# First loads in another order, a table of roots loaded at once, and the first product put between the transposes

## The reference, cut to what matters

```python
def rms_norm(x, g):
    xf = x.astype(jnp.float32)
    y = xf * lax.rsqrt(jnp.mean(xf * xf, axis=-1, keepdims=True) + EPS)
    return (y * g.astype(jnp.float32)).astype(x.dtype)
...
        h = rms_norm(x, norm_mix_pre[l])
        proj = h @ w_in[l]
        q, k, v, u, gates = jnp.split(proj, splits, axis=-1)
        q = q.reshape(b, s, ATTN_HEADS, HEAD_DIM)
        k = k.reshape(b, s, ATTN_HEADS, HEAD_DIM)
```

## Time and profile before

| | us |
|---|---|
| median of 3 runs | 1713.24 |
| lowest and highest | 1712.49, 1714.06 |
| the profiled execution, its own time | 1714.25 |
| its span, first to last instruction | 1712.4 |
| PE busy | 1585.0 (93%) |
| PE weight loads | 1120.9 (65%) |
| DVE busy | 723.9 (42%) |
| ACT busy | 532.1 (31%) |
| POOL busy | 164.0 (10%) |

### The profile page before, as it was taken

One profiled execution on the slowest core, in us unless ns is written; L12 is line 12 of the kernel. 1 busy time (PEld: TensorE's weight loads), 2 busy tenths in 40 slices (PEclk: granted clock), 3 DMA queues, 4 the chain that ended last, 5 costly groups with the idle time before them and its releaser, 6 DMA issues. The chain is left out here.

```text
span 1712.4 us, 19999 instructions
## 1 busy us (share of the span) xinstructions
PE 1585.0 (93%) x7970; PEld 1120.9 (65%) x7970; DVE 723.9 (42%) x1235; ACT 532.1 (31%) x911; POOL 164.0 (10%) x169
## 2 busy tenths in 40 slices
PE   4999899898999999998999788969999999999969
PEld 4766588788888888876766676744445444543449
DVE  4343422445444444476555676432122222212363
ACT  4333422244423323343454467221111111100242
POOL 0012201001111111102200210021000000000000
PEclk8999999999999999998999999989999999999989
DMA  6011222212221322312100221538999999999811
GB/s 253 31 68 55 101 109 99 101 60 111 83 93 71 123 99 74 114 71 98 50 25 29 95 99 50 204 154 335 419 421 421 421 421 420 418 418 421 352 39 47
DMA packets 44846, 302.85 MB, mean 177 GB/s; under 512 B 5056, under 2 KB 7232, under 8 KB 9680
## 3 DMA queue, kind: packets, MB, share of 16 engines
q1 hardware_dynamic: 42624, 294.12, 43.1%
q0 software_dynamic: 2128, 7.42, 1.3%
HBM read 299.43 MB, written 2.10 MB: 176 GB/s over the span
## 5 line engine op out<-in xcount | busy, mean ns | idle before, releaser
L580 DVE TENSOR_TENSOR w_lo<-M,w_hi 128x2048 fp32r<-128x2048 f32 x73 | 167.6, 2301 | 216.7 <-ACT w_hi L575 216.7
L2264 PE MATMUL bank<-M 128*64 128x512 f32 x1024 | 227.5, 595 | 5.7 <-DMA M<-in_w 4.7
L575 ACT ACTIVATE w_hi<-M 128x2048 fp32r<-128x2048 f32 x73 | 138.9, 1910 | 175.5 <-PE bank L748 63.6
L748 PE MATMUL bank<-HTH,w_hi 128*128 128x512 f32 x432 | 168.9, 391 | 5.2 <-DVE M L1266 5.2
L748 PE MATMUL bank<-HTL,w_hi 128*128 128x512 f32 x432 | 168.8, 391 | 0.0
L748 PE MATMUL bank<-HTH,w_lo 128*128 128x512 f32 x432 | 168.7, 390 | 0.0
L2264 PEld LDWEIGHTS bank<-M 128*64 128x64 f32 x1024 | 72.5, 137 | 139.9 <-issue 138.7
L770 PE MATMUL bank<-w_hi,HTH 128*128 128x512 f32 x256 | 106.3, 415 | 19.4 <-DVE M L1482 5.3
L2281 PE MATMUL bank<-M 128*64 128x512 f32 x512 | 113.8, 595 | 2.2 <-DMA M<-in_w 2.2
L770 PE MATMUL bank<-w_hi,HTL 128*128 128x512 f32 x256 | 102.7, 401 | 0.0
L770 PE MATMUL bank<-w_lo,HTH 128*128 128x512 f32 x256 | 102.6, 401 | 0.0
(11 more groups left out here) (312 smaller groups left out, 2940.3 us busy)
## 6 DMA issues: line engine op xcount, KB each, us to landing
M<-in_w SPq DMA_DIRECT2D x192, 1024.0 KB, 10.4
M<-in_wd SPq DMA_DIRECT2D x78, 1024.0 KB, 4.8
M<-in_nb SPq DMA_DIRECT2D x4, 1536.0 KB, 7.1
X<-in_x SPq DMA_DIRECT2D x4, 512.0 KB, 7.5
M<-in_rows POOLq DMA_DIRECT2D x4, 512.0 KB, 5.7
M<-in_tb POOLq DMA_DIRECT2D x8, 256.0 KB, 4.0
rowb<-in_rows POOLq DMA_DIRECT2D x4, 512.0 KB, 4.1
out<-M SPq DMA_DIRECT2D x16, 128.0 KB, 1.8
```

The source lines that it names most:

```text
L575: e.activation(hi[:, :], slots[slot_of[n]], ACT.Copy).then_inc(split_hi_done, 1)
L580: e.tensor_tensor(lo[:, :], slots[slot_of[n]], hi[:, :], ALU.subtract).then_inc(split_lo_done, 1)
L748: m = e.matmul(out[:, :], w[:, k0 + k, n0:n0 + 128], v[k], start=(k == 0 and i == 0), stop=(k == len(hi) - 1 and i == 2))
L2264: m = e.matmul(b[64 * s:64 * s + 64, :], Xe[:, 4 * kh + k, o + C * s:o + C * s + C], unit_w(key, 4)[:, k, :], start=(kh == 0 and k == 0), ...
```

## The change

There are four edits, all in the first stage.

- **Loads.** eps is moved next to the identity, and these 129 columns get a load of their own, right behind x0, with a semaphore of their own (`d_ident`). The first unit of weights is issued behind x1 and the second behind x3, ahead of the rest of `cst` and of `cols`. POOL issues the row of gains, then waits for x3, and only then issues the bias tables, `wpg`, `rows` and `wr`.
- **Table.** DVE sets a column to 1, and ACT takes its root ahead of everything else.
- **Order on ACT and DVE.** The stagger is written out: tiles 0 and 1 start together, the split of the first unit stands between the copies of tile 0 and those of tile 1, and tiles 2 and 3 come behind.
- **Order on PE.** Tiles 0 and 1 are transposed, then the q half of tokens 0 to 255 is made, then tiles 2 and 3 are transposed, then come the k half and the second half of the tokens. The banks of q and k are claimed ahead of those of tiles 2 and 3.

```diff
@@ sync, first loads
             for t in range(TT):
                 e.dma_start(X[:, t, :], x_d[t * 128:(t + 1) * 128, :]).then_inc(d_x[t], 16)
+                if t == 0:
+                    e.dma_start(cst[:, 0:NFIRST], cst_d[:, 0:NFIRST]).then_inc(d_ident, 16)
                 if t == 1:
-                    e.dma_start(cst[:, :], cst_d).then_inc(d_cst, 16)
-                    e.dma_start(cols[:, :], cols_d).then_inc(d_cols, 16)
+                    load_dense(e, 0)
+            load_dense(e, 1)
+            e.dma_start(cst[:, NFIRST:], cst_d[:, NFIRST:]).then_inc(d_cst, 16)
+            e.dma_start(cols[:, :], cols_d).then_inc(d_cols, 16)
...
         def first_loads_pool(e):
             load_gain(e, 0)
-            e.dma_start(wpg[:, :, :], wpg_d).then_inc(d_wpg, 16)
+            e.wait_ge(d_x[TT - 1], 16)
             for h in range(3):
                 load_tb(e, h)
+            e.dma_start(wpg[:, :, :], wpg_d).then_inc(d_wpg, 16)
...
+        one = stat()
+        FIRST_ACT = ((0, 0), (1, 0), (0, 3), "split", (1, 3), (2, 0), (3, 0), (2, 3), (3, 3))
+        FIRST_DVE = ((0, 1), (1, 1), (0, 4), "split", (1, 4), (2, 1), (3, 1), (2, 4), (3, 4))
+
         def pre_act(e):
-            for t, s in stagger(TT, 5, 2):
-                if t == 2 and s == 0:
+            e.wait_ge(one_set, 1)
+            act_own.mark(e.activation(one, one, ACT.Sqrt))
+            for step in FIRST_ACT:
+                if step == "split":
                     split_act(e, 0)
-                norm_act(e, 0, t, s)
+                else:
+                    norm_act(e, 0, *step)
             split_act(e, 1)
             split_act(e, 2)
...
         def pre_dve(e):
-            for t, s in stagger(TT, 5, 2):
-                if t == 2 and s == 1:
+            e.memset(one, 1.0).then_inc(one_set, 1)
+            for step in FIRST_DVE:
+                if step == "split":
                     split_dve(e, 0)
-                norm_dve(e, 0, t, s)
+                else:
+                    norm_dve(e, 0, *step)
...
         def pre_pe(e):
-            e.wait_ge(d_cst, 16)
-            for t in range(TT):
-                norm_pe(e, 0, t)
+            e.wait_ge(d_ident, 16)
+            norm_pe(e, 0, 0)
+            norm_pe(e, 0, 1)
...
             for half in range(2):
+                ts = slice(half * 256, (half + 1) * 256)
                 ht_ready(e, 0, 2 * half)
                 ht_ready(e, 0, 2 * half + 1)
-                gemm3_T_part(e, ("in", 0), outs, slice(half * 256, (half + 1) * 256), half == 1)
+                for j, (b, fills) in enumerate(outs):
+                    m = gemm3_T_some(e, ("in", 0), b, j, ts)
+                    if half:
+                        m.then_inc(fills, 1)
+                    elif j == 0:
+                        norm_pe(e, 0, 2)
+                        norm_pe(e, 0, 3)
```

More of the change, by code:

```diff
@@ L54 @@
 _o = 0
-for _n, _w in (("ident", 128), ("tri", 128), ("ones", 128), ("iota", 64), ("thr", 8), ("cnt", 64),
-               ("cos", 128), ("sin", 128), ("eps", 1)):
+for _n, _w in (("ident", 128), ("eps", 1), ("tri", 128), ("ones", 128), ("iota", 64), ("thr", 8), ("cnt", 64),
+               ("cos", 128), ("sin", 128)):
     CST[_n] = (_o, _w)
     _o += _w
-NCST = _o
+NCST, NFIRST = _o, 129
 def ffn_order():
@@ L221, in build @@
         d_x = [sem(f"d_x{t}") for t in range(TT)]
-        d_cst, d_cols, d_wpg, d_rows, d_rowb, d_wr, d_pT = (
-            sem(n) for n in ("d_cst", "d_cols", "d_wpg", "d_rows", "d_rowb", "d_wr", "d_pT"))
+        d_ident, d_cst, d_cols, d_wpg, d_rows, d_rowb, d_wr, d_pT = (
+            sem(n) for n in ("d_ident", "d_cst", "d_cols", "d_wpg", "d_rows", "d_rowb", "d_wr", "d_pT"))
         d_tb = [sem(f"d_tb{i}") for i in range(3)]
@@ L230, in build @@
         r_sq, r_sqrt, r_y, xadd = (sem(n) for n in ("r_sq", "r_sqrt", "r_y", "xadd"))
-        d_gain = sem("d_gain")
+        d_gain, one_set = sem("d_gain"), sem("one_set")
         u_zero, pooled, mix_hi = sem("u_zero"), sem("pooled"), sem("mix_hi")
@@ L251, in build @@
         for t in range(TT):
+            if t == 2:
+                for name in ("q", "k"):
+                    ps.put((name, 0))
             for h in range(2):
                 ps.put(("n", 0, t, h))
-        for name in ("q", "k"):
-            ps.put((name, 0))
         ATT = [(h, qt) for h in range(8) for qt in range(4)]
@@ L763, in gemm3_T_part, with gemm3_T_some @@
                     m.then_inc(fills, 1)
+        def gemm3_T_some(e, key, out, j, ts):
+            wh, wl = parts(key, KD)
+            for k in range(KD):
+                for i, (w, src) in enumerate(((wh, HTH), (wh, HTL), (wl, HTH))):
+                    m = e.matmul(out[:, ts], w[:, k, j * 128:(j + 1) * 128], src[:, k, ts],
+                                 start=(k == 0 and i == 0), stop=(k == KD - 1 and i == 2))
+            return m
         def gemm3_tok(e, key, j, t, out):
@@ L2443, in _ @@
                 first_loads_sp(e)
-                for n in range(NDENSE - 2):
+                for n in range(2, NDENSE - 2):
                     load_dense(e, n)
@@ L2806, in _layout @@
     one = np.ones((128, 1))
-    cst = np.concatenate([np.eye(128), np.triu(np.ones((128, 128)), 1), np.ones((128, 128)),
+    cst = np.concatenate([np.eye(128), one * EPS, np.triu(np.ones((128, 128)), 1), np.ones((128, 128)),
                           one * np.arange(64)[None, :], one * (C * (1 + np.arange(8)))[None, :], one * cnt,
-                          by_tok(np.cos(ang)), by_tok(np.sin(ang)), one * EPS], axis=1).astype(np.float32)
+                          by_tok(np.cos(ang)), by_tok(np.sin(ang))], axis=1).astype(np.float32)
     wr = np.concatenate([i["w_rg_2"][0], i["w_re_2"][0]], axis=1).reshape(8, 128, 36).transpose(1, 0, 2)
```

## The result

The changed kernel takes 1703.61 us (median of 9 runs, 1702.34 to 1711.82) against 1713.26 for the kernel before (9 runs, 1711.51 to 1721.20): ratio 0.9944, interval 0.9927 to 0.9962, which is 9.65 us less (6.5 to 12.5). Timed again (5 runs against 9), the ratio was 0.9960 (0.9946 to 0.9975), 6.9 us less (4.3 to 9.3).

What follows compares the result with a forecast made beforehand. The first stage up to the copy of k was taken to bound the start, with the gain row landing last. That copy moves from 41.5 to 35.4, so 1713.24 - 6.1 = 1707.1 us, range 1704.0 to 1710.6.

Steps and rivals of the forecast that it cites:

- The transfers: First loads: identity lands at about 4.9, x1 at 5.6, gain row at 8.45, first weights at 11.0 instead of 18.02.
- S: Start of tile 0's scaling on DVE, forecast at 8.5, right after the gain row lands.
- ACT and DVE: Norm and weight split ahead of the product: tile 0 scaled from 8.5, first matmul at 18.15 instead of 28.05.
- P: Start of the first matmul of the q and k product on PE, forecast at 18.15 instead of 28.05.
- PE, the step that failed: Product to k copy: first group 4.9, 16 transposes 3.5, three fast groups 8.64; k copied at 35.4.
- K: Start of DVE's copy of k, after which attention starts; forecast at 35.4 instead of 41.5, 6.1 us less.
- early rival: First stage: gain row lands with x1 (6.5), split waits for weights at 11.0, clock never falls; 1703.6, chance 0.06.
- No cost of the moves: First loads and banks: POOL's wait, later constants and swapped banks delay nothing; tables cost zero unless 14 us later.
- Passed through: After the copy of k: nothing later is tied to the program's start, so the whole 6.1 us reaches the end.
- identity no earlier: First loads: small load no quicker than the old table, ACT starts at 9.33, all 2.6 later; 1709.7, chance 0.04.
- given back: Later stages: expert weights arrive at a fixed rate, the gain ends in PE's wait for them; 1713.2, chance 0.04.
- slower: First loads: one queue's loads served side by side, first weights land at 24.5; 5.9 slower, 1719.1, chance 0.03.

Runs made afterwards that it cites:

- POOL at once: Changed kernel with POOL's wait for x3 and its new order of `wpg` taken back; k copied at 34.31 us in its profile, no whole time given.

## Why the prediction was wrong, point by point

- **The transfers**: first weights forecast at 11.0, landed at 10.7 to 11.8 in the four profiles of the changed kernel. The identity was forecast at 4.9 and was there at 4.3 in the first profile, 0.3 behind x0 (issued at 0.75, 3.3 to landing). Gain row forecast to end last, at 8.45: it did, S 8.49 on average. x1 was forecast at 5.6 and landed at 8.3 to 9.3: wrong. In the kernel before it was there at 5.4, issued 0.5 sooner and with the rate at 377 GB/s up to 5 us; here the rate was 221 from 4 to 5 us and 295 from 5 to 6. That this is the cause is likely, not shown. It cost nothing, as DVE waits for the gain row first.
- **ACT and DVE**: P was forecast at 18.15, S + 9.65; it came at S + 9.48, at 17.97 on average. Each step of that chain, with its length from before, holds.
- **PE, the step that failed**: from P to K the sum had 4.9 + 3.5 + 8.64 + the tail, 17.25. It takes 15.15. Nearly all of it is one term: "The 16 transposes come at 0.20 to 0.22 each at either clock". They take 1.66 or 1.67 in all four profiles, not 3.5, once the clock is up: 1.84 of the 2.1 us. The rest is the first group, 4.6 on average against 4.9. The premise came from the earlier trace rows, where 16 transposes at a shown clock of 1.00 were each no quicker than the 8 at 0.50. The view shows 1.00 until the first change it has a record of; the clock was low there as well, so the prediction's reading that it was at 2.4 GHz during those transposes and fell later does not hold for them. The matmuls of the same rows showed a halving from 0.21 to 0.12 apart, and an operation of the same engine that does not halve should have been suspected. The first group took 4.2 in the first profile (12 slow matmuls), 4.5 to 4.9 in the others: the 4.9 was at the upper end. Its low bound of 4.2 rested on no row of before.
- **The sum**: 6.1 + 2.1 for this stretch (1.84 of it the transposes) + 0.1 for P and K of before = 8.3, the mean of the profiles. The rest of the way to 9.65 is most likely chance: the first profile had the best landing and the best clock of four, the interval of 9.65 reaches down to 6.5, and the second timed comparison gave 6.9.
- **The range** took 1.2 us for the clock and 1 for the landings. The early rival, 1703.6, named both a higher clock and an early gain row, but priced the first at matmuls alone and left transposes out. That its time is the measured one is luck: the gain row came at 8.5 on average, not 6.5, and the first group ran mostly at the low clock.
- **No cost of the moves**: right. POOL's wait, the later constants and the swapped banks show in no wait of the first stage; tile 3's low copy ended at 25.0, 0.8 before the third group did (covered by 1.4 in the forecast).
- **Passed through**: right as far as the runs can tell. Span less K is the same within its own spread, and PE's wait for expert weights in the line of the earlier trace rows is 4.3 to 5.9 us after, 4.3 and 4.7 before; but the spread of some 5 us leaves room for a microsecond or two given back.
- The rivals "identity no earlier", "given back" (of the whole gain) and "slower" did not happen: identity at 4.35, K 8.3 earlier and the whole time 9.65 and 6.9 less, first weights landed 10.7 to 11.8 with the later loads behind them.

## What to carry to other kernels

At the start of a program, make out the clock from the spacing of instructions, not from the granted clock alone, and price every PE operation in the stretch at both levels. When a wait is taken away, look for the transfer that is next (here the gain row), and judge edits by marks relative to it, since its landing varies by about as much (1.5 us over four profiles) as an edit is worth (1.0 to 2.4). Filling PE's idle start with throw-away work takes about 2 us off the first stage here, but only while it ends before the real work is ready.

## What the runs showed of the hardware

- The granted clock reads 1.00 from the start of the span until the first recorded change, also while PE runs at 1.2 GHz. POOL at once, windows of 1 us with the product's first group in them, and two of its matmuls:

```profile
20.00:21.00 1.00, 1.00 (x6) 1.00 (x6) 0.90 (x3) 0.07 (x1) 0.00 (x0) 1.00 1.04 419
21.00:22.00 1.00, 1.00 (x7) 1.00 (x6) 0.97 (x1) 0.00 (x0) 0.00 (x0) 1.00 1.04 424
```

```profile
21.04 0.42 PE L771 MATMUL bank<-HTH,w_lo 128*128 128x256 f32 x1
21.25 0.42 PE L771 MATMUL bank<-HTH,w_hi 128*128 128x256 f32 x1
```

  Starts 0.21 apart are 256 columns at 1.2 GHz (256 / 1.2 = 213 ns); at 2.4 GHz they stood 0.12 apart in the same run from 22.9 on. The Trainium skill (TensorE: Matmul & The Clock Gate, What's actually happening) says that the throttled state is the default and that activity releases it; the trace agrees, by the spacing and not by the column.
- An fp32 transpose of 128 columns takes 0.20 to 0.21 us at 1.2 GHz (16 in 3.3 in the runs with all tiles turned first and with tiles 2 and 3 turned early) and 0.10 at 2.4 (16 in 1.66 in the changed kernel).
- One and the same order of transfers landed the gain row between 7.6 and 9.15 over four profiles of one kernel (7.05 to 9.55 over all variants with it on POOL's queue), whereas in two profiles of the kernel before it landed at 8.45 and 7.95, and the constants there at 9.33 and 9.20.
